# Fifteen strips of the next layer's modulation as dot products on VectorE, in place of five TensorE units among the first layer's heads

## The reference

```python
def encoder_layer(x, c, ...):
    mod = jax.nn.silu(c) @ w_ada + b_ada            # 1024 x 3072
    shift, scale, gate = jnp.split(mod, 3, axis=-1)
    h = rms_norm(x, ln_g) * (1.0 + scale[:, None, :]) + shift[:, None, :]
    # A: differential attention, 4 heads; B: 2-D neighbourhood attention, 4 x 2 heads;
    # C: dilated attention in three groups of 4 heads, mixed by their denominators
    ya, yb, yc = ...                                 # q, k normed (and roped in A, C) per head
    merged = sum(sigmoid(h @ w_g[i]) * ((y_i * silu(h @ w_z[i])) @ w_br[i]) for i, y_i in ...)
    return x + gate[:, None, :] * (merged @ w_out)
```

## Time and profile before

| | |
|---|---|
| time, median of 3 runs | 2335.7 us (2334.45 to 2336.24) |
| span of the profiled execution | 2334.2 us, 42068 instructions |
| timed median less profiled span | 1.5 us |
| TensorE, VectorE, ScalarE, POOL busy | 98%, 72%, 48%, 3% of the span |
| DMA | 198.72 MB, mean 85 GB/s |

### The profile page before, as it was taken

One profiled execution on the slowest core, in us unless ns is written; L12 is line 12 of the kernel. 1 busy time (PEld: TensorE's weight loads), 2 busy tenths in 40 slices (PEclk: granted clock), 3 DMA queues, 4 the chain that ended last, 5 costly groups with the idle time before them and its releaser, 6 DMA issues.

```text
span 2334.2 us, 42068 instructions
## 1 busy us (share of the span) xinstructions
PE 2289.5 (98%) x15370; PEld 2135.9 (92%) x15370; DVE 1669.9 (72%) x4593; ACT 1123.4 (48%) x3077; POOL 58.5 (3%) x103
## 2 busy tenths in 40 slices
PE   7999999999999999999999999999999999999999
PEld 5888889999998999999888899899999989999998
DVE  7877677777765766676578867777877667676772
ACT  5666565444444443344356765754444353343440
POOL 0010110000000000000001002100000000000000
PEclk9999999999999999999999999999999999999999
DMA  7221321111113243221521121121110223333223
GB/s 283 95 76 56 122 62 60 58 57 60 56 64 103 74 125 118 93 90 64 173 82 35 35 82 44 58 83 60 56 59 33 82 99 99 102 113 97 88 89 119
DMA packets 74556, 198.72 MB, mean 85 GB/s; under 512 B 10864, under 2 KB 31984, under 8 KB 71408
## 3 DMA queue, kind: packets, MB, share of 16 engines
q1 hardware_dynamic: 59232, 170.29, 21.7%
q10 hardware_dynamic: 15120, 25.74, 3.1%
HBM read 175.02 MB, written 18.87 MB: 83 GB/s over the span
## 4 chain that ended last, share of the span: by engine, by line
PE 81%; DVE 8%; ACT 4%; issue 3%; DMA 3%; SPq 0%; DVEq 0%; ACTq 0%
PE ps_proj L1046 51%; PE ps_score L1092 8%; PE ps_pt L1092 7%; PE ps_pt L1241 2%; PE ps_score L1225 2%; PE ps_pv L1277 2%; PE ps_score L1209 1%; PE ps_pv L1258 1%; PE ps_tr L1292 1%; DMA y_part<-parked 1%; PE ps_tr L1293 1%; PE ps_pv L1271 1%; DVE top L2120 1%; DMA first_ada<-in_w_first 1%; DMA s_raw<-in_w_gate 1%
## 5 line engine op out<-in xcount | busy, mean ns | idle before, releaser
L1046 PE MATMUL ps_proj<-w_hi,act_hi 128*128 128x384 f32 x1824 | 633.7, 347 | 2.2 <-ACT act_hi L1502 1.3
L1046 PE MATMUL ps_proj<-w_hi,act_lo 128*128 128x384 f32 x1824 | 612.7, 336 | 0.0
L1046 PE MATMUL ps_proj<-w_lo,act_hi 128*128 128x384 f32 x1824 | 612.4, 336 | 0.0
L1046 PEld LDWEIGHTS ps_proj<-w_hi,act_hi 128*128 128x128 f32 x1824 | 343.1, 188 | 7.3 <-ACT act_hi L1502 4.8
L1046 PEld LDWEIGHTS ps_proj<-w_lo,act_hi 128*128 128x128 f32 x1824 | 343.8, 188 | 0.0
L1046 PEld LDWEIGHTS ps_proj<-w_hi,act_lo 128*128 128x128 f32 x1824 | 342.9, 188 | 0.0
L2049 DVE TENSOR_REDUCE ssq<-square 128x2 f32<-128x256 f32 (+1 forms) x228 | 95.6, 419 | 207.0 <-ACT square L1600 206.4
L1600 ACT ACTIVATE square<-ps_proj 128x256 f32<-128x256 f32 x228 | 88.1, 387 | 263.8 <-PE ps_proj L1046 263.4
L2426 DVE TENSOR_TENSOR w_lo<-w_raw,w_hi 128x1536 fp32r<-128x1536 f32 (+3 forms) x105 | 169.2, 1612 | 22.3 <-ACT w_hi L1426 21.5
L1426 ACT ACTIVATE w_hi<-w_raw 128x1536 fp32r<-128x1536 f32 (+2 forms) x104 | 144.3, 1388 | 42.5 <-DMA w_raw<-in_w 19.7
L2338 DVE TENSOR_TENSOR s_lo<-s_raw,s_hi 128x512 fp32r<-128x512 f32 x224 | 150.9, 686 | 1.7
(11 more groups left out here) (263 smaller groups left out, 5089.8 us busy)
## 6 DMA issues: line engine op xcount, KB each, us to landing
w_raw<-in_w SPq DMA_DIRECT2D x80, 768.0 KB, 5.7
s_raw<-in_w_gate SPq DMA_DIRECT2D x96, 256.0 KB, 3.2
w_ada<-in_w_mod SPq DMA_DIRECT2D x11, 1536.0 KB, 6.7
w_raw<-in_w SPq DMA_DIRECT2D x24, 512.0 KB, 3.8
wb_raw<-in_w_branch SPq DMA_DIRECT2D x24, 512.0 KB, 3.6
first_ada<-in_w_first SPq DMA_DIRECT2D x8, 1024.0 KB, 12.7
w<-in_w_gate SPq DMA_DIRECT2D x32, 256.0 KB, 3.8
parked<-y_t ACTq DMA_DIRECT2D x4, 1536.0 KB, 5.1
```

Of the source, the lines that this page charges most:

```text
L1046: op = pe.matmul(out, sta[s](k), mov[m](k), start=(k == 0 and n == 0), stop=(k == chunks - 1 and n == 2))
```

## The change

The five units are taken out of the list. Their 15 strips become 30 dot products on VectorE, one for each strip and sequence: w_ada is laid out on the host so that partition p of a strip holds the 1024 weights of its output p, and silu(c), 1024 values for each sequence, is copied to all partitions. One `tensor_tensor_reduce` multiplies a strip by it and adds up, starting from the bias, and writes mod[:, s, r]. The remaining three modulation units of layer 0, and all of layer 1, stay.

- Hosts: the 39 units from A1,0 to B3,2 (`_hosts`); dot i stands at host i * 39 // 30, on VectorE behind `item_end` and ahead of `divisors`.
- silu(c) goes from c_wide to a DRAM buffer (silu_rows) by ScalarE's queue at unit A0,4, and back as a broadcast of 8 KB to 128 partitions (c_rows, 1 MB) at A0,5, where ScalarE waits for the store.
- Strips of 512 KB come by ScalarE's queue into three buffers; the first three right behind the broadcast, each later one at the position two units behind the dot that frees its buffer.
- c_rows, the strips and the product lie in `merged`.

```diff
+ADA_FIRST = (5, 0)
...
 def layer_units(l):
-    out, ada = [], [("a", l, e) for e in range(ADA_GROUPS[l])]
-
-    def head(kind, h, g=0, middle=False):
+    out, ada = [], [("a", l, e) for e in range(ADA_FIRST[l], ADA_GROUPS[l])]
+
+    def head(kind, h, g=0):
         for t in range(TILES):
             out.append(("q", l, kind, h, g, t))
-            if t == 1 and middle and len(ada) > 3:
-                out.append(ada.pop(0))
...
+STRIPS = 3 * ADA_FIRST[0]
+DOTS = [(s, g) for s in range(STRIPS) for g in range(2)]
+_hosts = range(AT["q", 0, "A", 1, 0, 0], AT["q", 0, "B", 3, 0, 3])
+DOT_AT = {d: _hosts[i * len(_hosts) // len(DOTS)] for i, d in enumerate(DOTS)}
+DOTS_IN = {n: [d for d in DOTS if DOT_AT[d] == n] for n in _hosts}
+STRIP_IN = {DOT_AT[s - 3, 1] + 2: s for s in range(3, STRIPS)}
...
+        c_rows = sb("c_rows", [P, D, 2], F32, t_at["merged"])
+        strips = [sb(f"strip{b}", [P, D], F32, t_at["merged"] + 4 * D * (2 + b)) for b in range(3)]
+        dot_prod = sb("dot_prod", [P, D], F32, t_at["merged"] + 4 * D * 5)
...
+            def load_strip(s):
+
+                if s >= 3:
+                    act.wait_ge(*dot_done.at((s - 3, 1)))
+                act.dma_start(strips[s % 3][:], w_strip[s]).then_inc(*strip_in[s % 3].inc(s))
+
+            def load_rows():
+
+                act.wait_ge(*xn_ready.at((0, 1, KC - 1)))
+                act.wait_ge(rows_kept, 16)
+                act.dma_start(c_rows[:].rearrange("p k g -> p (k g)"), silu_rows.rearrange("p k g -> (p k g)").partition_broadcast(P)).then_inc(rows_in, 16)
+                for s in range(3):
+                    load_strip(s)
...
                 if u == LAYER_UNITS[l][0]:
                     norm(l)
+                if u == ("q", 0, "A", 0, 0, JOINT):
+                    act.wait_ge(c_ready, 1)
+                    act.dma_start(silu_rows, c_wide[:, :, 0:2]).then_inc(rows_kept, 16)
+                if u == ("q", 0, "A", 0, 0, TILES - 1):
+                    load_rows()
+                if n in STRIP_IN:
+                    load_strip(STRIP_IN[n])
...
             def scale_gain(l):
                 dve.wait_ge(*mod_summed.at(("a", l - 1, ADA_GROUPS[l - 1] - 1)))
+                dve.wait_ge(*dot_done.at(DOTS[-1]))
...
+            def dot(s, r):
+
+                if (s, r) == DOTS[0]:
+                    dve.wait_ge(rows_in, 16)
+                if r == 0:
+                    dve.wait_ge(*strip_in[s % 3].at(s))
+                if r == 1:
+                    dve.wait_ge(*dot_done.at((s, 0)))
+                elif s > 0:
+                    dve.wait_ge(*dot_done.at((s - 1, 1)))
+                dve.memset(dot_fence[:], 0.0)
+                dve.tensor_tensor_reduce(dot_prod[:], strips[s % 3][:], c_rows[:, :, r], 1.0,
+                                         col[:, COL_ADA + 2 * s + r:COL_ADA + 2 * s + r + 1], ALU.mult, ALU.add,
+                                         mod[:, s, r:r + 1]).then_inc(*dot_done.inc((s, r)))
...
                 if u1 is not None and u1[0] == "q":
                     item_end(u1)
+                for d in DOTS_IN.get(n, ()):
+                    dot(*d)
                 if n in LOW_IN and u[0] == "a":
                     low_part(LOW_IN[n])
...
+    strips = np.stack([_strip(w_ada[1], s * P).transpose(2, 0, 1).reshape(P, D) for s in range(STRIPS)])
+    w = w[ADA_FIRST[0]:]
```

More of the change, by code:

```diff
@@ L116, in layer_units @@
 def layer_units(l):
-    out, ada = [], [("a", l, e) for e in range(ADA_GROUPS[l])]
-    def head(kind, h, g=0, middle=False):
+    out, ada = [], [("a", l, e) for e in range(ADA_FIRST[l], ADA_GROUPS[l])]
+    def head(kind, h, g=0):
         for t in range(TILES):
             out.append(("q", l, kind, h, g, t))
-            if t == 1 and middle and len(ada) > 3:
-                out.append(ada.pop(0))
[L125 to L129, removed]
+    for kind in "AB":
+        for h in range(HEADS):
+            head(kind, h)
     for h in range(HEADS):
@@ L146 @@
 AT = {u: n for n, u in enumerate(UNITS)}
+STRIPS = 3 * ADA_FIRST[0]
[4 more added lines that the diff above has]
+STRIP_IN = {DOT_AT[s - 3, 1] + 2: s for s in range(3, STRIPS)}
+assert len(STRIP_IN) == STRIPS - 3
 def joint(u):
@@ L409, in inc, with build @@
         return self.sem, self.unit
-def build(nc, x_in, c_in, w, w_gate, w_branch, w_mod, w_first, rows, cols, ada_first, rpb, ident_in, sum_in, rope_a, rope_c, mask_c, mask_s, mask_b, lam_c, y):
+def build(nc, x_in, c_in, w, w_gate, w_branch, w_mod, w_strip, w_first, rows, cols, ada_first, rpb, ident_in, sum_in, rope_a, rope_c, mask_c, mask_s, mask_b, lam_c, y):
     ctx = ExitStack()
@@ L512, in build @@
         parked = nc.dram_tensor("parked", (DEPTH * len(PARKED), P, HK, TOK), F32, kind="Internal").ap()
+        silu_rows = nc.dram_tensor("silu_rows", (P, KC, 2), F32, kind="Internal").ap()
         ident = sb("ident", [P, P])
@@ L548, in build @@
         fence = sb("fence", [P, 1])
+        dot_fence = sb("dot_fence", [P, 1])
         y_ss = sb("y_ss", [P, 3])
@@ L613, in build @@
         w_lo_ready = tally("w_lo_ready", SPLIT_ORDER)
-        mod_raw = tally("mod_raw", adas)
+        rows_kept = sem("rows_kept")
+        rows_in = sem("rows_in")
+        strip_in = [tally(f"strip_in{b}", range(b, STRIPS, 3), unit=16) for b in range(3)]
+        dot_done = tally("dot_done", DOTS)
         mod_summed = tally("mod_summed", adas)
@@ L994, in _ @@
                 if p[0] == "a":
-                    sp.dma_start(w_ada[b][:], w_mod[sum(ADA_GROUPS[:p[1]]) + p[2]]).then_inc(*w_in[b].inc(p))
+                    sp.dma_start(w_ada[b][:], w_mod[adas.index(p)]).then_inc(*w_in[b].inc(p))
                 else:
@@ L1533, in turn_out @@
                 else:
-                    if u[2] >= 2:
+                    if u[2] >= ADA_FIRST[u[1]] + 2:
                         act.wait_ge(*mod_summed.at((*u[:2], u[2] - 2)))
@@ L2600, in _ada_groups @@
                 w_ada[l + 1 if s < FIRST else l], s * P)
+    strips = np.stack([_strip(w_ada[1], s * P).transpose(2, 0, 1).reshape(P, D) for s in range(STRIPS)])
+    w = w[ADA_FIRST[0]:]
     first = np.stack([np.concatenate([_strip(w_ada[0], f * P) for f in (k, KC + k)], axis=2) for k in range(KC)])
-    return w, first
+    return w, strips, first
 def _cols(ln_g, b_ada, subln_a):
@@ L2660 @@
                                             lam_q1, lam_k1, lam_q2, lam_k2)], axis=1)
-    w_mod, w_first = _ada_groups(npy(w_ada))
+    w_mod, w_strip, w_first = _ada_groups(npy(w_ada))
     rows = np.pad(rows, ((0, 1), (0, 0)))
@@ L2667 @@
     lam_c = np.broadcast_to(np.stack([lam_init, 1.0 - lam_init], 1).astype(np.float32), (P, DEPTH + 1, 2))
-    data = dict(x_in=x_in, c_in=c_in, w=w, w_gate=w_gate, w_branch=w_branch, w_mod=w_mod, w_first=w_first, rows=rows, cols=cols,
+    data = dict(x_in=x_in, c_in=c_in, w=w, w_gate=w_gate, w_branch=w_branch, w_mod=w_mod, w_strip=w_strip, w_first=w_first, rows=rows, cols=cols,
                 ada_first=ada_first, rpb=rpb, ident_in=np.eye(P, dtype=np.float32),
```

## The result

The changed kernel takes 2340.5 us (median of 14 runs, 2338.57 to 2342.38), the kernel before on the same chip 2336.2. The ratio is 1.0019, 95% interval 1.0013 to 1.0026: slower by 0.2%, at the edge of what this measurement tells from no change. 2336 was predicted. The profiled execution has a span of 2339.9 us, 5.7 more than the profiled one of before; it is one of the longer of the 14, whose spans go from 2336.8 to 2340.6.

The account below looks back on a forecast made before the run. TensorE, busy 98% of the span, was taken to bound the kernel. Start +3.4, A1 to A3 +1.3 and B -4.0 sum to +0.7: span 2334.9, timed about 2336 us, own range 2330 to 2343.

Parts of the forecast that it names:

- The start: Layer 0 up to the A1 to A3 loops: store, broadcast and first dot add 3.4 us, ends +1 and +15.
- Rival 4: At the start the small store lands in 8 to 12 us, costing 5 to 9 more: 2341 to 2345; chance 7%.
- The other 2.4 of the start: VectorE before A1 to A3: first dot waits 1.0 us for broadcast and strip, and itself takes 1.4.
- the sum of the loops: VectorE's eighteen loops in A1 to A3: 109.8 us plus 14 dots, 19.0, make 128.8 against 124.6 today.
- my own refutation: The forecast is wrong if VectorE stays under 92% busy in A1 to A3, or a dot takes over 1.5 us.
- The row of 0.83 us: Tiny VectorE instruction beside POOL's bias building, 0.15 us elsewhere; taken to agree that two-SBUF-input VectorE instructions and POOL exclude each other.
- the lead of TensorE behind VectorE: At tile B0,0: 6.0 us now, to shrink to about 3 when VectorE sets the pace, giving back 3.0.
- The 3 us of new waits: B0 to B3: new waits, ends 0 and 9, making the part 149.8 us against 153.8, -4.0.
- The removal: Taking the five units out of layer 0's A and B parts can bring about 11.8 us at most.
- rival 1: VectorE hides all dots in A1 to A3 and B: 2325, in good part 2325 to 2331; chance 27%.
- rival 2: VectorE is overrun: dots wait for POOL, probability transposes wait on TensorE, and B gives nothing: 2345; chance 16%.
- rival 3: The strided read makes a dot 2.4 us, 1.0 more each: +22, 2358; chance 5%.

Follow-up runs that it names:

- compact store: Changed kernel, but ScalarE first copies silu(c) to a gapless tile and stores 128 pieces of 64 bytes instead of 1024 of 8; 2336.0 us, ratio 1.0001 to before.
- start aside: Changed kernel with the silu(c) store issued right behind the first norm and the broadcast and first strips at A0,3; 2334.9 us, ratio 0.9995 to before.
- the last: Against the kernel before: three of eight modulation units become 18 dots from A2,0 to B3,2, and bias tables load in B1 instead of A3; 2325.4 us, ratio 0.9951.
- removal alone: Changed kernel without dots, store, broadcast and strips, so five units are simply not computed; 2322.6 us, ratio 0.9946 to before.
- rows apart: All 30 dots from B0,0 to C0,1,5 and each sequence's 1024 silu(c) values contiguous, against the changed kernel; 2332.9 us, ratio 0.9987 to before.
- dots in B and C: Changed kernel with all 30 dots hosted from B0,0 to C0,1,5, store at A1,0 and broadcast at A3,0; 2331.7 us, ratio 0.9982 to before.

## Why the prediction was near in time and wrong in a step

**The start failed.** "pieces so small are not shown. Ends of the landing 2 and 12 us, I take 3": it was 6.8. This is the term that was mis-sized, 1.0 us for TensorE where first scores are 5.1 later. Rival 4 named this, with 5 to 9 more and 2341 to 2345, and had 7%: the 4.1 on top of the forecast lie just under its lower end, and 2340.5 beside its 2341. The row I leaned on for 3 was of 256 KB in large pieces; the bytes were 32 times fewer, but cut into 1024 pieces, and the compact store shows that this is what cost. The Trainium skill ("DMA: Bandwidth & Descriptors", Specifications) says that below 512 bytes a DMA reads, modifies and writes. It pointed the right way, but the compact store's pieces of 64 bytes are below that too and landed in 1.4 us, so this line alone would not have given the price. The other 2.4 of the start came out at +2.35 by luck: I had put 1.0 there for a wait of the first dot, which was 0.16, and nothing for the scores at half clock, which was 0.85. The start aside, whose scores run at full clock, has 1.5 behind its first scores.

**A1 to A3: the sum of the loops was near by errors that cancel, and what follows from it was not right.** 128.8 us were forecast and 127.0 measured. 5.1 of these were waits for ScalarE that the sum did not have; fourteen dots displace 1.20 each and not 1.36, 2.2 less; and so the loops without dots and waits take 105.1 where I had 109.8. VectorE was to be over 95% busy, and was 92%, on the border of my own refutation: the slower engine's own work did not fill the time, since it stood for ScalarE in turn. The row of 0.83 us that I put beside the rule on two SBUF inputs has only one; the one at 125.27 above has two. And the lead of TensorE behind VectorE did not shrink: 5.96 us after 6.0. The 3.0 that were to come back at the end of A3 did not come in any kernel; in the last the lead is 3.8, but there POOL's work had made VectorE's last loop 2.6 longer. So A gave +2.4 for +1.3. Of the signs, the 145 us from the first scores to B0,0 came (145.0), and VectorE's delay did reach TensorE's "ps_pt", but for the scaled output (6.8 us) more than for the probabilities (1.6).

**B** gave 5.7 of the 7.0 that the removal alone brings; 4.0 were forecast, and 150 for the part against 148.1. The 3 us of new waits were 1.3. **The rest** held within 1 us.

**The removal** was put at 11.8; alone it gives 12.3 in A and B and 1.5 more behind them, and 12.6 timed (ratio 0.9946, its interval 9.3 to 15.7).

**Sum.** Over the five stretches +3.5 instead of +0.7: on top of the forecast the start gave +4.0, A +1.1, B -1.7 and the rest -0.7; timed it is +4.3. The time lies in the stated range because B and the rest made good part of the start.

**Rivals.** All hidden (rival 1) fell: fifteen dots in A cost 7.4 of 18.0 us. Overrun (rival 2) fell too: POOL's work makes one loop in A 2.6 longer, but B gave most of its part. The slow strided read (rival 3) fell at 1.28.

Where did the gain go? Of 17 to 18 us between the removal alone and the change, 7.4 went to the transfers and the waits for them, and about 10 to the products, most of that in A (7.4).

## What to carry to other kernels

Offload to a second engine only up to what its stage has free. Read that from a loop with its waits, not from the busy share: in the B part, beside a VectorE busy 74%, ten dots were free, fourteen cost 1.0 us and twenty 5.3, and in A, beside 84%, fifteen cost two fifths of their time. And before moving a few kilobytes through memory, count the pieces: here a copy into a dense tile brought the landing from 6.8 us to 1.4 and the first scores 3.8 us forward.

## What the runs showed of the hardware that was not expected

- A store of 8 KB from SBUF in 1024 pieces of 8 bytes: issue 0.59 us, landing 6.8 in the kernel after, 5.7 to 8.6 over the others, and 16.8 beside large loads; over 10 to 15 us 236 GB/s were moved there, for 391. In 128 pieces of 64 bytes 0.34 and 1.4.
- TensorE's clock did not fall by the length of a wait alone, and a fall did not always cost. In the compact store it fell to half at a wait of 2.68 us, and one loop of VectorE was 0.9 longer; in the kernel after the wait of 2.56 at the same place in the order left it at 1.00. Behind the first scores' wait of 5.0 it made the scores 0.85 longer. In rows apart it was low for half as long as in dots in B and C, with the same waits, and the B part was no shorter.
- The accumulator's read behind a multiply-reduce (0.09 us) and, where it does not wait, the fence ahead of it (0.06) lie wholly beside their neighbours on VectorE.
